# Prompt attention: the product with the values as one plain fp32 matmul per key block

## The reference, cut to what matters

```
p_c = masked_softmax(s, ...);  o_c = einsum('bqghn,bngd->bqghd', p_c, cv)
p_s = masked_softmax(...);     o_s = einsum('bqghm,bqgmd->bqghd', p_s, v_selected)
p_w = masked_softmax(...);     o_w = einsum('bqghk,bkgd->bqghd', p_w, v_window)
o = g[..., 0:1] * o_c + g[..., 1:2] * o_s + g[..., 2:3] * o_w
```

## Time and profile before

| | us |
|---|---|
| runs of the kernel (3) | 2175.88, 2179.14, 2182.30 |
| median | 2179.14 |
| span of the profiled execution | 2176.1 |
| prompt attention in it, from the first scores to the last drain (490.11 to 841.30) | 351.2 |

### The profile page before, as it was taken

How to read it: one execution, slowest core, us unless ns; L and a number is a source line. 1 busy time by engine, 2 the same in 40 slices (tenths; PEclk the granted TensorE clock), 3 DMA queues, 4 the chain that set the end, 5 groups by cost and what they waited for, 6 DMA issues and landing times. The chain is left out here.

```text
span 2176.1 us, 26887 instructions
## 1 busy us (share of the span) xinstructions
PE 1901.2 (87%) x9884; PEld 1595.6 (73%) x9884; DVE 1056.7 (49%) x1919; ACT 841.6 (39%) x1704; POOL 186.7 (9%) x336
## 2 busy tenths in 40 slices
PE   5996975768889997879959997799999999999997
PEld 4896863557667775748648862699998999988886
DVE  4532245546677875364344532544445544454444
ACT  4311222325666665241145521443334433343332
POOL 0001102113333321010000000000000000000000
PEclk8997987777899998969959998899999999999999
DMA  5415304210000002230030001533434333343431
GB/s 192 177 37 114 104 1 126 89 37 1 1 1 1 1 1 85 75 137 1 7 123 39 1 27 70 175 116 117 139 130 145 117 134 137 116 161 139 145 125 63
DMA packets 109977, 185.21 MB, mean 85 GB/s; under 512 B 18416, under 2 KB 79280, under 8 KB 109799
## 3 DMA queue, kind: packets, MB, share of 16 engines
q1 hardware_dynamic: 89759, 156.84, 21.1%
q0 software_dynamic: 8144, 25.40, 3.6%
q10 hardware_dynamic: 11968, 1.58, 0.6%
HBM read 175.30 MB, written 12.73 MB: 86 GB/s over the span
## 5 line engine op out<-in xcount | busy, mean ns | idle before, releaser
L2414 DVE TENSOR_TENSOR mlp_dn_lo<-mlp_dn_raw,mlp_dn_hi 128x1024 fp32r<-128x1024 f32 x96 | 117.6, 1225 | 315.6 <-ACT mlp_dn_hi L2342 315.6
L2266 PE MATMUL mlp_psU<-mlp_xT_hi,mlp_up_hi 128*128 128x384 f32 (+1 forms) x768 | 254.0, 331 | 5.3 <-DVE mlp_up_lo L2408 5.3
L2266 PE MATMUL mlp_psU<-mlp_xT_hi,mlp_up_lo 128*128 128x384 f32 (+1 forms) x768 | 252.2, 328 | 0.0
L2266 PE MATMUL mlp_psU<-mlp_xT_lo,mlp_up_hi 128*128 128x384 f32 (+1 forms) x768 | 252.1, 328 | 0.0
L2281 PE MATMUL mlp_acc<-mlp_dn_hi,mlp_h_hi 128*128 128x512 f32 (+1 forms) x576 | 224.5, 390 | 0.0
L2281 PE MATMUL mlp_acc<-mlp_dn_lo,mlp_h_hi 128*128 128x512 f32 (+1 forms) x576 | 224.4, 390 | 0.0
L2281 PE MATMUL mlp_acc<-mlp_dn_hi,mlp_h_lo 128*128 128x512 f32 (+1 forms) x576 | 224.1, 389 | 0.0
L2342 ACT CAST mlp_dn_hi<-mlp_dn_raw 128x1024 fp32r<-128x1024 f32 x96 | 100.5, 1047 | 281.3 <-PE mlp_acc L2281 281.3
L2266 PEld LDWEIGHTS mlp_psU<-mlp_xT_hi,mlp_up_hi 128*128 128x128 f32 x768 | 145.2, 189 | 11.2 <-issue 3.3
L2266 PEld LDWEIGHTS mlp_psU<-mlp_xT_lo,mlp_up_hi 128*128 128x128 f32 x768 | 145.2, 189 | 3.3
L2266 PEld LDWEIGHTS mlp_psU<-mlp_xT_hi,mlp_up_lo 128*128 128x128 f32 x768 | 145.1, 189 | 0.0
(11 more groups left out here) (405 smaller groups left out, 4008.6 us busy)
## 6 DMA issues: line engine op xcount, KB each, us to landing
mlp_up_raw<-in_w_up SPq DMA_DIRECT2D x48, 1024.0 KB
mlp_dn_raw<-in_w_down SPq DMA_DIRECT2D x48, 1024.0 KB
cross_mem<-in_cache_mem_kv SPq DMA_DIRECT2D x8, 1024.0 KB, 4.9
qkv_w_raw<-in_w_in SPq DMA_DIRECT2D x8, 652.0 KB, 5.8
mem_w_raw<-in_w_mkv SPq DMA_DIRECT2D x8, 512.0 KB, 4.8
cmp_raw<-in_cache_cmp_kv SPq DMA_DIRECT2D x32, 128.0 KB
cmp_raw<-in_cache_cmp_kv POOLq DMA_DIRECT2D x32, 128.0 KB, 6.2
smp_sel<-in_cache_sel_kv SPq DMA_DIRECT2D x32, 128.0 KB
```

The costliest lines, as they stand in the source:

```text
L2266: m = nc.tensor.matmul(psU[n % 2][:, 0:w], a[:, u % 2, c, :], b[:, g % 2, c, 0:w], start=(c == 0 and n_pass == 0), stop=(c == KC - 1 and n ...
L2414: nc.vector.tensor_tensor(dn_lo[:, u % 2], dn_raw[:, k, a, :], dn_hi[:, u % 2].bitcast(F32), ALU.subtract).then_inc(s_dl, 1)
```

## The change

Each key block now has one plain fp32 matmul: stationary are the 64 value columns as they stand in `yq` (or `cv_p`, now 64 columns), moving is the copy `pT` of the transposed probabilities, 128x512, no longer rounded. The tiles `v_st`, `pT_hi`, `pT_lo` and `other` and the instructions that filled them are gone. The bank is copied once, by ACT for even block numbers and by DVE for odd ones. `psO` has 64 rows; in the drain ACT copies the odd heads straight into `aT`, and DVE the even heads behind it. The order of the steps is the same.

```
-                    val = cv_p[0:NCMP, g, :] if branch == 2 else v_st[:, branch, kb, g, :]
-                    pe.wait_ge(s_th, n + 1)
+                    c_v = C_KS + branch * KVW + NG * HD + g * HD
+                    val = cv_p[0:NCMP, g, :] if branch == 2 else yq[:, kb, c_v:c_v + HD]
+                    pe.wait_ge(*copied(n))
                     if arg == 0 and u:
-                        pe.wait_ge(s_od, u)
+                        pe.wait_ge(s_ov, u)
                     out = psO[:, :, :].rearrange("p a b -> p (a b)")
-                    nc.tensor.matmul(out, val, pT_hi[0:rows, n % (LAG + 1), :], start=(arg == 0), stop=False)
-                    pe.wait_ge(s_tl, n + 1)
-                    m = nc.tensor.matmul(out, val, pT_lo[0:rows, n % (LAG + 1), :], start=False, stop=last)
+                    m = nc.tensor.matmul(out, val, pT[0:rows, n % (LAG + 1), :], start=(arg == 0), stop=last)
...
+        def copied(n):
+            return (s_tv, n // 2 + 1) if n % 2 else (s_ta, n // 2 + 1)
...
-                            v = yq[:, i, C_KS:C_KS + 2 * KVW].rearrange("p (b u g d) -> p b u g d", b=2, u=2, g=NG)[:, :, 1]
-                            nc.scalar.copy(v_st[:, :, i, :, 0:HD], v).then_inc(s_vh, 1)
...
-                        act.wait_ge(s_pt, n + 1)
-                        nc.scalar.copy(pT_hi[0:w, n % (LAG + 1), :], bank[kind, arg][0:w].rearrange("p a b -> p (a b)")).then_inc(s_th, 1)
+                        if n % 2 == 0:
+                            act.wait_ge(s_pt, n + 1)
+                            nc.scalar.copy(pT[0:w, n % (LAG + 1), :], bank[kind, arg][0:w].rearrange("p a b -> p (a b)")
+                                           ).then_inc(s_ta, 1)
...
-                        if u:
-                            act.wait_ge(s_od, u)
-                        halves = psO[:, :, :].rearrange("p (m e) t -> p e m t", e=2)
-                        nc.scalar.copy(other[0:HD], halves[HD:P, 0])
-                        nc.scalar.copy(other[HD:P], halves[0:HD, 1]).then_inc(s_oc, 1)
+                        nc.scalar.copy(aT[HD:P, 2 * g:2 * g + 2, i * P:(i + 1) * P],
+                                       psO[:, :, :].rearrange("p (m e) t -> p e m t", e=2)[:, 1]).then_inc(s_oa, 1)
...
-                        dve.wait_ge(s_th, n + 1)
-                        nc.vector.tensor_tensor(pT_lo[0:w, n % (LAG + 1), :], bank[kind, arg][0:w].rearrange("p a b -> p (a b)"),
-                                                pT_hi[0:w, n % (LAG + 1), :].bitcast(F32), ALU.subtract).then_inc(s_tl, 1)
+                        if n % 2:
+                            dve.wait_ge(s_pt, n + 1)
+                            nc.vector.tensor_copy(pT[0:w, n % (LAG + 1), :], bank[kind, arg][0:w].rearrange("p a b -> p (a b)")
+                                                  ).then_inc(s_tv, 1)
...
-                        dve.wait_ge(s_oc, u + 1)
-                        halves = psO[:, :, :].rearrange("p (m e) t -> p e m t", e=2)
-                        dst = aT[:, 2 * g:2 * g + 2, i * P:(i + 1) * P]
-                        nc.vector.tensor_tensor(dst[0:HD], halves[0:HD, 0], other[0:HD], ALU.add)
-                        nc.vector.tensor_tensor(dst[HD:P], halves[HD:P, 1], other[HD:P], ALU.add).then_inc(s_od, 1)
+                        dve.wait_ge(s_oa, u + 1)
+                        nc.vector.tensor_copy(aT[0:HD, 2 * g:2 * g + 2, i * P:(i + 1) * P],
+                                              psO[:, :, :].rearrange("p (m e) t -> p e m t", e=2)[:, 0]).then_inc(s_ov, 1)
```

More of the change, by code:

```diff
@@ L614, in _ @@
                 nc.scalar.copy(ck_hi[:, :, :], psP[:, 0, :, :])
-                nc.scalar.copy(cv_p[0:NCMP, :, 0:HD], psP[0:NCMP, 1, :, :])
+                nc.scalar.copy(cv_p[0:NCMP, :, :], psP[0:NCMP, 1, :, :])
                 nc.scalar.copy(cv_s[:, 0:4, :], psV[0][:, :, :])
@@ L663, in _ @@
                 nc.vector.tensor_copy(ck_s[:, :, :], psT[0][:, :, :].rearrange("p a b -> p (a b)").rearrange("p (b n) -> p b n", b=DB))
-                nc.vector.tensor_tensor(ck_lo[:, :, :], psP[:, 0, :, :], ck_hi[:, :, :].bitcast(F32), ALU.subtract)
-                chain(nc.vector.tensor_tensor(cv_p[0:NCMP, :, HD:P], psP[0:NCMP, 1, :, :],
-                                              cv_p[0:NCMP, :, 0:HD].bitcast(F32), ALU.subtract))
+                chain(nc.vector.tensor_tensor(ck_lo[:, :, :], psP[:, 0, :, :], ck_hi[:, :, :].bitcast(F32), ALU.subtract))
 N_SEL = PAST + DT
@@ L1097, in prompt_attention @@
         k_lo = ph.sb("k_lo", [P, 2, NG, SEQ], F32R)
-        v_st = ph.sb("v_st", [P, 2, n_tiles, NG, P], F32R)
         prob = ph.sb("prob", [P, 2 * HPG, P_COLS])
         stat = ph.sb("stat", [P, 2 * HPG, 16])
-        pT_hi = ph.sb("pT_hi", [P, LAG + 1, 4 * P], F32R)
-        pT_lo = ph.sb("pT_lo", [P, LAG + 1, 4 * P], F32R)
-        other = ph.sb("other", [P, 2, P])
+        pT = ph.sb("pT", [P, LAG + 1, 4 * P])
         psA = ph.ps("psA", [P, 2, 512])
@@ L1106, in prompt_attention @@
         psT = [ph.ps(f"psT{k}", [P, 4, P]) for k in range(3)]
-        psO = ph.ps("psO", [P, 4, P])
+        psO = ph.ps("psO", [HD, HPG, P])
         flatA = psA[:, :, :].rearrange("p a b -> p (a b)")
@@ L1126, in prompt_attention @@
         s_ql = ph.sem("prep_lo_made")
-        s_vh = ph.sem("value_hi_made")
         s_sa = ph.sem("sel_scores_made")
@@ L1137, in prompt_attention @@
         s_pt = ph.sem("probs_transposed")
-        s_th = ph.sem("pT_hi_made")
-        s_tl = ph.sem("pT_lo_made")
+        s_ta = ph.sem("pT_copied_by_scalar")
+        s_tv = ph.sem("pT_copied_by_vector")
         s_o = ph.sem("unit_output_made")
-        s_oc = ph.sem("other_halves_copied")
-        s_od = ph.sem("output_drained")
+        s_oa = ph.sem("odd_heads_drained_by_scalar")
+        s_ov = ph.sem("even_heads_drained_by_vector")
         s_dve = ph.sem("vector_chain")
@@ L1152, in prompt_attention @@
                 bank[kind, arg] = psT[len(drained) % len(psT)]
-                drained.append((s_tl, base[arg[0]] + arg[1] + 1) if kind == "block" else (s_ql, prep_no(arg) + 1))
+                drained.append(copied(base[arg[0]] + arg[1]) if kind == "block" else (s_ql, prep_no(arg) + 1))
         with nc.Block() as block:
@@ L1338, in _ @@
                         w = NCH if key_blocks(u)[b][1] == 2 else P
[L1339 to L1340 removed]
+                        if n % 2 == 0:
+                            act.wait_ge(s_pt, n + 1)
+                            nc.scalar.copy(pT[0:w, n % (LAG + 1), :], bank[kind, arg][0:w].rearrange("p a b -> p (a b)")
+                                           ).then_inc(s_ta, 1)
                     elif kind == "drain":
                         u = arg[0]
+                        i, g = units[u]
                         act.wait_ge(s_o, u + 1)
[L1344 to L1348 removed]
+                        nc.scalar.copy(aT[HD:P, 2 * g:2 * g + 2, i * P:(i + 1) * P],
+                                       psO[:, :, :].rearrange("p (m e) t -> p e m t", e=2)[:, 1]).then_inc(s_oa, 1)
             @block.vector
@@ L2595, in build @@
             ck_lo = ph.sb("ck_lo", [P, NG, NCH], F32R)
-            cv_p = ph.sb("cv_p", [HD, NG, P], F32R)
+            cv_p = ph.sb("cv_p", [HD, NG, HD])
             with ExitStack() as c4:
```

4 lines of the change are left out of this document (removed).

## The result

The changed kernel takes 2200.37 us (median of 4 runs, 2197.04 to 2202.35) against 2180.72 for the kernel before (4 runs): the ratio is 1.0082, with a 95% interval of 1.0060 to 1.0105. It is 0.8% slower.

The account below looks back on a forecast made before the run. PE was taken to set the pace late in the prompt attention. The terms 53 + 32 + 5 - 42 - 6 = +42 us, on the span of 2176.1 with the median 3.0 above it, gave 2221 us; range 2184 to 2250.

Parts of the forecast that it names:

- What bounds the kernel now: Prompt attention, 351.2 us: PE is nearest to full and sets the pace late; its idle time is taken as 47 us.
- dearer product, tiles 0 to 2: Early query tiles' share of the plain fp32 product's extra PE time, 0.40 + 0.24 us a full block: +17 us.
- dearer product, tiles 3 to 7: Late query tiles' share of the plain fp32 product's extra PE time, 0.40 + 0.24 us a full block: +72 us.
- idle time and clock together: Prompt attention: PE's idle time given back, -42 us, and less half clock, -6 us; -48 us in all.
- no stall at the change of width: Rival, value product: 64 columns among 128 cost no stall, so the 32 us drop out; 2189 us (2177 to 2201), chance 0.18.
- Streaming and width changes: Value product, 132 full blocks: plain fp32 streaming adds 0.40 us each, +53; stalls at column width changes 0.24 each, +32.
- The idle time: PE's waits in prompt attention: one copy and longer products cover them except at drains, -42 us (bounds -47 and -20).
- the handoff was the pace: Rival, prompt attention: transposes, ACT copy, DVE subtraction and free bank set the pace; shortening gives -14 us, 2165 us, chance 0.08.
- The clock: Prompt attention's last three stretches: PE's half clock partly rises to full, -6 us (bounds -20 and +8).
- Compressed blocks and the drain: 16 compressed blocks' products 0.3 us dearer each, +5 us; waits for the last copy at 16 drains keep 5 us idle.
- the signs that I had named for a wrong forecast: Late product under about 0.9 us of PE, score waits unchanged, or the stage's mean granted clock moving over 0.05.

Follow-up runs that it names:

- The wide product: The changed kernel with the 128 value columns of both groups stationary in the plain fp32 product instead of 64: 2172.19 us, ratio 0.9949 to the kernel before.

## Why the forecast was right and wrong

**What bounds the kernel now** named PE late in the stage, and the sum then let PE set the pace of the whole of it. That is the step that failed: the forecast priced a block at 0.40 + 0.24 and charged it 132 times, in the tiles 0 to 2 as well, where the dearer product costs nothing. 24 of those blocks (and 6 compressed ones) belong to the tiles 0 to 2, 17 us of the forecast. There PE's work for the product of a block, reckoned at full clock, was 0.23, 0.46, 0.86, 0.92 and 1.15 us in five kernels with one copy, and the units 1 to 5 took 74.8, 76.2, 75.6, 75.7 and 76.1; with two steps it was 0.46, 0.92 and 1.15, and they took 88.5, 88.0 and 87.0. What moved them is the copy, and with it the work of DVE and ACT: 60.94 to 50.16 and 53.87 to 44.16 us busy, 10.8 and 9.7 less, in a stretch that became 12.4 shorter. Neither is full there, and what DVE is idle for is ACT, so they go at the pace at which they hand work to each other. The experiments change the number of copies and the length of that chain together; which of the two counts, and which link comes last, they do not separate.

The sign of it could be seen beforehand. In the earlier trace rows the second stretch has PE busy 72.51 of 87.63 us at a clock of 0.84, so it was idle for 15 us and at half clock for 28. I read the low clock as a cost to be won back; in these units a higher clock won nothing back, because PE was not the bound.

Part by part, in us of the stage:

| step of the forecast | forecast | measured | by |
|---|---|---|---|
| dearer product, tiles 0 to 2 | +17 | 0 | pair and plain, one copy |
| dearer product, tiles 3 to 7 | +72 | +62.8 | the same, 210.36 to 273.14 |
| shorter handoff (idle time and clock), tiles 0 to 2 | not parted | -12.2 | two steps and one, fp32r pair |
| shorter handoff, tiles 3 to 7 | not parted | -25.0 | the same |
| idle time and clock together | -48 | -37.2 | sum of the last two rows |
| sum | +42 | +25.5 | |

The measured column takes one of two orders, the copy first and then the product. In the other order (the product first, with two steps) the dearer product is -1.5 and +45.7 us and the shorter handoff -10.9 and -7.9. In both the product costs nothing in the tiles 0 to 2; in the tiles 3 to 7 only the sum of the two, +37.8, is free of the order.

The stage accounts for 16.5 of the 22 us between the loss that was forecast (42) and the one measured (20). The other 6 lie outside it: the stage grew by 25.5 us in the profiled executions and the median by 20. The code there is the same, and in those two executions 4 us of it lie behind the stage; the cause is open. As a time alone, 2200 us fits the rival "no stall at the change of width" (2177 to 2201) better than the forecast (2203 to 2240). The trace shows the stall all the same, 0.29 us a block, so the time by itself would have confirmed the wrong mechanism.

**Streaming and width changes.** The price of streaming was right, 0.86 us; that of the width was somewhat small, 0.24 for 0.29. It rested on less than it said: two of its rows show 0.09, and the third shows 0.13 for both ends together. That the late total is 62.8 and not 108 x 0.69 + 10 x 0.3 = 78 comes at least in part from slack that longer products fill: with one copy PE was idle for 14.1 us of these units with the pair (210.36 - 196.29) and for 4.2 with the plain product, and of the 27 us that one product saves there only 12.3 show.

The Trainium skill, "TensorEngine Tiling (Array Packing)", Key Properties, says that a change of the tiling mode drains the engine. If a product of 64 columns among 128 is such a change, the trace agrees for the plain product (0.29 a block, gone with 128) and not for the fp32r product.

**The idle time**, -42 by covered waits and a shorter handoff, is near the -37.2 of the table and far from the -18.8 of the other order, so its size is partly luck. In the early units it went by the wrong reason: there the copies paced the stage, as the rival "the handoff was the pace" said. DVE's wait for ACT's copy, which that rival named (35.2 of the 37.2 us in the earlier trace rows are for ACT), was the sign, and 13.1 of it lie in units 1 to 5. The rival put its turning point at 0.97 us a product. The wide product, 0.86, is faster than the kernel before, and the narrow one, 1.15, is slower, as its condition has it; on a line between their two stages (346.7 and 376.7 us) the 351.2 of the kernel before lies at about 0.90, an estimate. Its sum still let PE's work count in every tile, and its 2165 us for 0.86 was 2172.

**The clock**, -6 "in the middle" between -20 and +8, was a term that should not have stood there for the tiles 0 to 2. For the late units its 2 + 7 us were for half clock that went, as the mean rose from 0.96 to 1.00; but with the late code of the kernel before 0.99 was no faster than 0.96, so no run shows that it was worth anything there either.

**Compressed blocks and the drain** are too small to be told apart in these runs. Of the signs that I had named for a wrong forecast, one came: the mean clock of the stage moved by more than 0.05 (0.90 to 0.97).

## What to carry to other kernels

Before you charge an engine's extra work to the time, ask stretch by stretch whether that engine is the bound there. A stretch in which it waits and its clock is low may take added work for nothing and give little back if you lighten it, as units 1 to 5 did. Adding work to one engine in one stretch is a cheap experiment that answers this before the real change is written. And try a plain fp32 product in the column width of its neighbours, even if half of its columns are thrown away: here that was worth 28 us.

## What the runs showed of the hardware

- A plain fp32 matmul with 64 stationary columns between matmuls with 128 costs 0.29 us more per block than one with 128 (1.59 and 1.30 us from product to product at full clock); an fp32r matmul with 64 columns in the same place costs nothing more (2138.88 us, and 2141.10 with 128).
- In units 1 to 5 TensorE's granted clock was 0.85 before, 0.92 with two more fp32r products in each block, 1.00 with four fp32r products or with the plain one of 64 columns on a single copy, and 0.86 with one product. More work did not always go with a higher clock: the wide product on a single copy had 0.95 in one kernel and 1.00 in another. A higher clock shortened nothing there (88.48 us at 0.85 and 88.01 at 0.92; 74.83 at 0.86 and 76.09 at 1.00).
- The part ahead of the stage, the same in all these kernels, ended between 488 and 497 us in single profiled executions. Spans of single executions can't tell a few us; stretches of the stage can (77.39, 76.09 and 75.71 us, or 88.48, 88.41 and 88.01, in kernels with the same handoff there).
